# The sigmoid of two gate quarters in the merge: ScalarE's Ln and Exp, or VectorE's reciprocal

## The reference, cut to what matters

```python
N_BRANCH = 5           # D_MODEL = 1024, SEQ = 256, BRANCH_WIDTH = 512
...
up = jnp.einsum('bsnw,nwd->bsnd', ys, w_up)
merged = jnp.sum(jax.nn.sigmoid(gates.reshape(b_, s_, N_BRANCH, D_MODEL)) * up, axis=2)
out = merged @ w_out
return x + rms_norm_2(out, norm_post)
```

## Time and profile before

| | us |
|---|---|
| median of 3 runs | 2239.56 (2237.78 to 2240.24) |
| the profiled execution's own time | 2238.56 |
| its span, from first to last instruction | 2236.8 |
| TensorE busy | 1907.9 (85%) |
| VectorE busy | 945.0 (42%) |
| ScalarE busy | 372.3 (17%) |

### The profile page before, as it was taken

How to read it: one execution, slowest core, us unless ns; L and a number is a source line. 1 busy time by engine, 2 the same in 40 slices (tenths; PEclk the granted TensorE clock), 3 DMA queues, 4 the chain that set the end, 5 groups by cost and what they waited for, 6 DMA issues and landing times. The chain is left out here.

```text
span 2236.8 us, 24556 instructions
## 1 busy us (share of the span) xinstructions
PE 1907.9 (85%) x10222; PEld 1144.2 (51%) x10222; DVE 945.0 (42%) x1509; ACT 372.3 (17%) x751; POOL 0.2 (0%) x4
## 2 busy tenths in 40 slices
PE   8999886667767667766667999999999999999998
PEld 5687842233323322322223787774446787874445
DVE  7758431121111122122222354477663264577762
ACT  1123300000000000000001222113323222123332
POOL 0000000000000000000000000000000000000000
PEclk9999998988997999898889999999999999999999
DMA  7222799999999999999998334435433433336330
GB/s 272 100 84 100 284 395 428 427 427 428 428 428 427 428 427 427 427 428 428 428 429 357 137 151 169 125 133 213 186 120 131 151 151 137 136 113 254 150 150 20
DMA packets 44824, 594.77 MB, mean 266 GB/s; under 512 B 5455, under 2 KB 6640, under 8 KB 8824
## 3 DMA queue, kind: packets, MB, share of 16 engines
q1 hardware_dynamic: 42808, 584.29, 64.1%
q10 hardware_dynamic: 1920, 9.09, 1.3%
HBM read 590.20 MB, written 1.06 MB: 264 GB/s over the span
## 5 line engine op out<-in xcount | busy, mean ns | idle before, releaser
L1997 PE MATMUL ps<-ring,arena 128*32 128x512 f32 x2032 | 289.4, 704 | 176.3 <-DMA ring<-in_w_experts 168.1
L613 PE MATMUL ps<-arena,ring 128*128 128x256 f32 x1792 | 399.9, 378 | 1.0 <-DVE arena L1164 0.8
L613 PEld LDWEIGHTS ps<-arena,ring 128*128 128x128 f32 x1792 | 333.7, 189 | 50.1 <-issue 3.4
L807 PE MATMUL ps<-ring,arena 128*128 128x512 f32 x656 | 286.4, 592 | 0.0
L1997 PEld LDWEIGHTS ps<-ring,arena 128*32 128x32 f32 x2032 | 62.1, 119 | 375.4 <-DMA ring<-in_w_experts 209.4
L807 PEld LDWEIGHTS ps<-ring,arena 128*128 128x128 f32 x656 | 124.5, 190 | 155.1 <-issue 155.0
L2027 PE MATMUL ps<-ring,arena 128*32 128x256 f32 x2016 | 139.2, 423 | 48.8 <-DMA ring<-in_w_experts 39.3
L2641 DVE COPY arena<-ps 128x256 f32<-128x256 f32 x64 | 27.2, 425 | 246.6 <-PE ps L2027 246.6
L2027 PEld LDWEIGHTS ps<-ring,arena 128*32 128x32 f32 x2016 | 64.8, 120 | 113.2 <-DMA ring<-in_w_experts 50.9
L2631 DVE TENSOR_TENSOR arena<-arena,ps 128x512 f32<-128x512 f32 x16 | 11.0, 688 | 231.6 <-PE ps L1997 231.6
L1698 PE MATMUL ps<-arena,ring 128*128 128x272 f32 x448 | 107.0, 393 | 0.0
(11 more groups left out here) (439 smaller groups left out, 2080.7 us busy)
## 6 DMA issues: line engine op xcount, KB each, us to landing
ring<-in_w_experts SPq DMA_DIRECT2D x190, 2048.0 KB, 26.4
ring<-in_w_layers SPq DMA_DIRECT2D x64, 2048.0 KB, 7.8
ring<-in_w_first SPq DMA_DIRECT2D x9, 2048.0 KB, 7.8
early<-in_w_layers SPq DMA_DIRECT2D x6, 2048.0 KB, 8.4
arena<-in_w_mem SPq DMA_DIRECT2D x4, 2048.0 KB, 19.3
ring<-in_w_first SPq DMA_DIRECT2D x4, 512.0 KB, 6.6
early<-in_w_experts SPq DMA_DIRECT2D x1, 2048.0 KB, 28.2
arena<-in_w_experts SPq DMA_DIRECT2D x1, 2048.0 KB, 9.6
```

Source lines behind the costliest of these rows:

```text
L613: last = pe.matmul(ps[:, j % 2, 0:SEQ], t[:, s, k, :], lhs[:, k, :], start=(k == 0), stop=(k == KD - 1))
L807: last = pe.matmul(ps[:, bank, :], lhs[:, k, :], rhs[:, k, :], start=(first and k == 0), stop=(k == n - 1), skip_group_check=True)
L1997: last = pe.matmul(ps[CAP * e:CAP * (e + 1), v // 4, :], xg[:, (v % 4) * 2 + k, CAP * e:CAP * (e + 1)], w[:, k, e, :], start=(v % 4 == 0 a ...
```

## The change

`bound` on VectorE no longer caps quarters 0 and 1 (`g11`, `g22`); it adds 1 to the exp and takes the reciprocal, and says so on a new semaphore, `gate_d`. ScalarE's two `sigmoid` calls for them are gone, four of its instructions for each branch. `gather` of these quarters waits for `gate_d`. Quarters 2 and 3 (`g12`, `g21`) are as before, with new counts. TensorE's and SyncE's programs are not touched.

```diff
                 def sigmoid(b, i, tile):
-                    w("gate_m", Q, 4 * b + i + 1)
+                    w("gate_m", 2 * NBR, 2 * b + i - 1)
                     link(act.activation(tile, tile, ACT.Ln, bias=ones[:, 0:1]))
                     act.activation(tile, tile, ACT.Exp, scale=-1.0).then_inc(sem("gate_r"), 1)
...
                     act.copy(g21, ps[:, G_BANK[0], :]).then_inc(sem("gate_c"), 1)
-                    sigmoid(b, 0, g11)
                     w("up_prod", G, 7 * b + 3)
...
                     act.activation(g22, g22, ACT.Exp, scale=-1.0).then_inc(sem("gate_e"), 1)
-                    sigmoid(b, 1, g22)
                     w("gate_prod", G, 7 * b + 6)
...
                 def bound(b, i, tile):
                     w("gate_e", Q, 4 * b + i + 1)
+                    if i < 2:
+                        link(dve.tensor_scalar(tile, tile, 1.0, None, ALU.add))
+                        dve.reciprocal(tile, tile).then_inc(sem("gate_d"), 1)
+                        return
                     dve.tensor_scalar(tile, tile, 1e18, None, ALU.min).then_inc(sem("gate_m"), 1)

                 def gather(b, i, out, g, u):

-                    w("gate_r", Q, 4 * b + i + 1)
+                    if i < 2:
+                        w("gate_d", 2 * NBR, 2 * b + i + 1)
+                    else:
+                        w("gate_r", 2 * NBR, 2 * b + i - 1)
```

## The result

| | before | after |
|---|---|---|
| median of 20 runs each, us | 2238.0 (2234.95 to 2241.7) | 2242.39 (2239.97 to 2245.48) |
| profiled execution's own time | 2238.56 | 2244.47 |
| its span | 2236.8 | 2242.7 |

The ratio is 1.0019, 95% interval 1.0013 to 1.0025: 4.3 us slower, between 2.9 and 5.6. That is inside the 0.2% that I called no change, with little to spare, and twenty runs of each kernel do tell it from zero.

What follows compares the result with a forecast made beforehand. It took an unbroken piece of TensorE products, 175.10 us in either merge, to bound the kernel. Stalls of 0.15 + 1.4 = 1.55 us a merge, 3.1 us in all, on 2239.56 gave 2242.7 us, range 2240.4 to 2248.0.

Steps and rivals of the forecast that it cites:

- The reciprocal: VectorE's new 128x512 reciprocal for g11 and g22: 3353 ns each, upper bound 3488 ns.
- Its successor: VectorE's next instruction, needing nothing of the reciprocal, starts 3.27 us behind it; a pair takes 3.73 us.
- VectorE's round: VectorE's time for a branch becomes 36.60 us, 0.55 us longer than TensorE's.
- P14: TensorE product waiting for the add of u22 behind g22's reciprocal: a stall of about 0.15 us in branch 0.
- The leads left in branches 1, 2 and 3: VectorE's time in hand at P14: 1.6, 1.1 and 0.5 us, so no stall there.
- P4 of branch 4: TensorE product waiting for ScalarE's copy of g11: next tightest place, about 1 us left.
- The second turn: TensorE's second turn after branch 4: g22's chain 2.56 us later, 1.17 us spare, a stall of 1.4 us.
- The sum of a merge: Stalls at P14 of branch 0 and the second turn: 0.15 + 1.4 = 1.55 us a merge, 3.1 us in all.
- ScalarE's relief: Ln and Exp removed for 20 quarters on ScalarE: costed at nothing, since nobody on the chain waits for them.
- VectorE sets the pace: Rival: TensorE waits at P14 of branches 0, 2 and 3; 6.6 us slower or more; chance 0.20.
- All is hidden: Rival: the delays at P14 and the turns are covered or taken up, 2239.6 us; chance 0.09.
- Faster: Rival: ScalarE's lighter load shortens something on the chain, perhaps 1 us, 2238.5 us; chance 0.03.

Runs made afterwards that it cites:

- early cap: Changed kernel with g12's cap in branch 4 directly behind g22's reciprocal, ahead of the add of u22 and g22's gather; ratio to before 1.0004.
- eighteen pairs: Changed kernel with g22 of the last branch back on ScalarE, 18 of 20 pairs on VectorE; ratio to before 0.9997.
- the turn alone: Kernel before with only g22 of the last branch on VectorE's reciprocal, 2 pairs; ratio to before 1.0015.
- 64 more columns: Changed kernel plus a useless 128x64 reciprocal behind g11's reciprocal in every branch; ratio to before 1.0039.
- g11 alone: Changed kernel with only g11 on VectorE's reciprocal, g22 back on ScalarE; ratio to before 0.9999.
- g22 alone: Changed kernel with only g22 on VectorE's reciprocal, g11 back on ScalarE; ratio to before 1.0012.

## Why the prediction was right, point by point

**Forecast and sum.** 2242.7 us against 2242.39. That closeness is luck: the median of before was forecast from three runs at 2239.56 and is 2238.0 over twenty, so the start was 1.6 us too high; the difference came out at +4.3 (2.9 to 5.6) where I had +3.1, 1.2 us too small; the two errors nearly cancel. By the profiles the two merges lost 3.4 us; the other 0.9 us of the medians' difference lies inside its interval, and no run ties it to a place.

**The reciprocal.** I took 3353 ns from the row of the same shape and measured 3354. So the upper bound (3488) was not needed. My estimate of 4.27 us, for which I read the "repeat count of 8" of the Trainium skill (VectorE: DVE Perf Modes, "the 8-slice pipeline in each mode") as eight cycles an element, disagrees with this measurement too.

**Its successor.** I let it start 3.27 us behind. It does where it needs nothing of it: in the rows of the early cap, 1681.85 - 1678.58 = 3.27.

**VectorE's round.** Forecast 36.60 us. VectorE's timeline has the reciprocals of g11 in branches 2 and 3 at

```profile
1595.69 3.35 DVE L1418 RECIPROCAL arena<-arena 128x512 f32<-128x512 f32 x1
...
1632.31 3.35 DVE L1418 RECIPROCAL arena<-arena 128x512 f32<-128x512 f32 x1
```

which are 36.62 us apart. VectorE's busy time in a middle branch was forecast at 32.6 us and is 32.30.

**P14.** In branch 0 I had the add of u22 start at 1540.60 and P14 begin 0.15 us late. Taken back by the 2.27 us by which this merge starts later, the add starts at 1540.55; it ends at 1543.45 in the rows below, 0.06 us before P14 begins, and P14 is 0.10 us late:

```profile
1539.55 3.35 DVE L1418 RECIPROCAL arena<-arena 128x512 f32<-128x512 f32 x1
1542.82 0.63 DVE L1412 TENSOR_TENSOR arena<-ps,arena 128x512 f32<-128x512 f32 x1
```

The leads left in branches 1, 2 and 3 were forecast at 1.6, 1.1 and 0.5 us; the add of u22 ends 1.46, 0.89 and 0.32 us before P14. So they were each 0.14 to 0.21 us too large, and the point from which VectorE paces lay at 0.32 us more over three rounds, not 0.5. At P4 of branch 4, where I had about 1 us left, ScalarE's copy of g11 ended 0.8 us before its time.

**The second turn.** From the first instruction on g22's exp to its gather I had 4.45 us. VectorE's timeline, the answer to the earlier trace rows:

```profile
1680.57 0.43 DVE L1417 TENSOR_SCALAR arena<-arena 128x512 f32<-128x512 f32 x1 [1.48 <-ACT arena L1119]
1681.04 3.35 DVE L1418 RECIPROCAL arena<-arena 128x512 f32<-128x512 f32 x1
1684.31 0.63 DVE L1412 TENSOR_TENSOR arena<-ps,arena 128x512 f32<-128x512 f32 x1
1685.04 0.69 DVE L1440 TENSOR_TENSOR arena<-arena 128x512 f32<-128x512 f32 x1
...
1686.37 0.42 DVE L1420 TENSOR_SCALAR arena<-arena 128x512 f32<-128x512 f32 x1
1688.25 0.69 DVE L1440 TENSOR_TENSOR arena<-ps,arena 128x512 f32<-128x512 f32 x1 [1.46 <-ACT arena L1090]
1688.98 0.69 DVE L1447 TENSOR_TENSOR ring<-ring,arena 128x512 f32<-128x512 f32 x1
```

1685.04 - 1680.57 = 4.47 us. The last add starts 8.41 us behind the first row, where it was 5.82: 2.59 later, less the 1.17 spare, and 0.05 for the handoff to TensorE, which I had left out, makes the 1.47 us of the timeline. I had 1.4. g22's own cap was on no critical path before; that its delay passes through g12, a quarter whose arithmetic was not changed, was the point to find.

**The sum of a merge was 0.17 us short**, 1.55 for 1.72. The step that was mis-sized is that an arrival late by so much costs so much. P14 was 0.10 us late, and its merge 0.20 longer (early cap, and eighteen pairs); the turn alone was 1.48 late and its merge 1.54 longer; with 64 more columns 0.69 + 0.71 + 1.06 + 1.48 = 3.94 us late became 4.30. So each of these restarts of TensorE adds 0.06 to 0.10 us to the lateness, and the lateness itself was forecast at 1.55 and is 0.10 + 1.47 = 1.57.

**ScalarE's relief is worth nothing**: right. With g11 alone, ScalarE was spared ten pairs and the merges stayed at 191.46 us.

**The rivals.** *VectorE sets the pace* was the right second case: the place (P14 of branches 0, 2 and 3) came out with 64 columns, half a microsecond more in each branch. The point at which it begins was not run for; the leads measured at P14 (above) put it at 0.32 us. Its price was low: I had 0.65 in branch 0, 1.0 in branch 3 and 1.65 at the turn, 3.3 us a merge, where the lateness was 0.69, 0.71 (branch 2), 1.06 and 1.48, and the merges 4.30 and 3.97 longer. Branch 2 was missing, from the leads that I had too large, and the restarts. *All is hidden* had as one way that the turns' delay is taken up in front of the output product; the 0.67 us of waiting for the copy stayed whole behind the late turn, since the copy moves along. *Faster* had nothing: the kernels with g11 alone and with the early cap are level with the kernel before at best.

## What to carry to other kernels

An engine that is busy 42% could take on 65 us more of work nearly unseen here (0.4 us in all with the early cap), but only where its consumers have a lead: look for the last stage, in which the engine has caught up and each of its instructions stands in a chain up to the engine that paces. There, ask what is queued behind the slower operation: here the loss came through g12's cap, an instruction that was not changed, and issuing it ahead of the add and the gather took the loss away. And since the work was moved off an engine that TensorE did not wait for, the best result at hand was no change; the microseconds lay in a wait (0.68 us for a copy behind the last turn) that other work could be put in front of.

## What the runs showed of the hardware that I had not expected

**A restart costs more than the lateness.** TensorE late by 0.10 us at P14 of branch 0 made the merge 0.20 longer. The other 0.10 us lies behind P14's start: the 44 instructions from there take 19.15 us behind a wait (64 columns) and 19.05 where P14 is on time (g22 alone). In the kernel after, P14's first instruction is recorded with 0.70 us where it was 0.59 before, and the next starts 0.53 us behind it in place of 0.43. At the second turn the extra is 0.06 us. At the copy behind the last turn it lies behind the start up to which the merge is measured. From that start to the last output product the kernel before takes 20.61 us and the one with the last turn moved 20.50, so that kernel gains 0.94 us a merge and not 0.84. No run shows why a first instruction takes longer.

**Recorded idle is shorter than the lateness**: 1.31 against 1.47 us at the second turn, 0.68 against 0.83 at the copy (due at 1695.29 + 0.44, begun at 1696.56). The difference is that the four matmuls in front are recorded with 0.60 us where the next would start 0.44 behind their start; a matmul's recorded end is modelled. In every wait looked at here, the idle in the profile was less than what its removal gave.

**Narrow reciprocals keep their rate.** 494 ns for 64 columns and 895 for 128, beside 3354 for 512: 401 ns for the first 64 columns more, 6.3 ns a column, and 6.4 from 128 to 512. The fixed part is small (some 0.1 us), so an estimate by columns would have held.

**Behind a reciprocal an independent instruction is recorded shorter**: the add of u22 takes 0.63 us where it took 0.68, g12's cap 0.36 where it took 0.42. Its start lies 0.08 us before the reciprocal's recorded end, as with other instructions. No run shows what this is.
